# Modulation products moved out of an input phase, a convolution carried on by chunks, and transposes between projection products, in a four-layer Trainium2 kernel

## The reference

```
shift, scale, gate = split(silu(c) @ w_mod + b_mod)
h = rms_norm(x, g) * (1 + scale) + shift
x = x + gate * fn(h)
```

```
b_gate, c_gate, u = split(h @ w_in, 3)
v = c_gate * u
conv[t] = w[2]*v[t] + w[1]*v[t-1] + w[0]*v[t-2]      (per channel)
return (b_gate * conv) @ w_out
```

## Time and profile before

| | |
|---|---|
| median of 3 runs | 2230.7 us (2225.03 to 2233.52) |
| the profiled execution: time, span | 2235.24 us, 2233.4 us |
| TensorE busy, mean granted clock | 1965.2 us (88%), 0.916 |
| VectorE busy | 1664.8 us (75%) |
| ScalarE busy | 1143.7 us (51%) |
| DMA | 551.03 MB, mean 247 GB/s |

### The profile page before, as it was taken

One profiled execution on the slowest core, in us unless ns is written; L12 is line 12 of the kernel. 1 busy time (PEld: TensorE's weight loads), 2 busy tenths in 40 slices (PEclk: granted clock), 3 DMA queues, 4 the chain that ended last, 5 costly groups with the idle time before them and its releaser, 6 DMA issues.

```text
span 2233.4 us, 29567 instructions
## 1 busy us (share of the span) xinstructions
PE 1965.2 (88%) x9224; PEld 1633.4 (73%) x9224; DVE 1664.8 (75%) x2294; ACT 1143.7 (51%) x1600; POOL 36.5 (2%) x47
## 2 busy tenths in 40 slices
PE   2968999877799999999999999585779998678998
PEld 2956887656678888888888888564768877466886
DVE  7877666967498989898898989675676668566554
ACT  2434444333277777777777777424344443434443
POOL 2000000000000000000000000000000000000000
PEclk9988999876699999999999999786689998679999
DMA  7965873964189999999999999373457866435662
GB/s 266 363 204 187 263 250 121 335 201 164 57 287 339 368 337 364 336 350 354 340 362 338 366 337 368 134 248 91 134 178 260 261 209 207 112 112 160 216 208 85
DMA packets 368358, 551.03 MB, mean 247 GB/s; under 512 B 35715, under 2 KB 292998, under 8 KB 368230
## 3 DMA queue, kind: packets, MB, share of 16 engines
q1 hardware_dynamic: 353120, 542.56, 71.9%
q10 hardware_dynamic: 14278, 6.70, 2.2%
q0 software_dynamic: 832, 0.30, 0.1%
HBM read 548.38 MB, written 1.08 MB: 246 GB/s over the span
## 4 chain that ended last, share of the span: by engine, by line
PE 75%; DVE 14%; DMA 5%; issue 3%; ACT 2%; SPq 0%; ACTq 0%; POOL 0%; DVEq 0%; POOLq 0%
PE ps L381 21%; PE ps L383 21%; PE ps L382 21%; PE ps L773 2%; DVE mod_acc L1370 2%; PE ps L919 2%; DVE units_low L376 2%; DMA raw_units<-in_w_in 1%; PE ps L827 1%; PE ps L762 1%; PE ps L750 1%; DMA raw_units<-in_attn_w_qkv 1%; DVE x_tokens L1396 1%; DMA raw_units<-in_conv_w_in 1%; DVE x_normed L1395 1%
## 5 line engine op out<-in xcount | busy, mean ns | idle before, releaser
L376 DVE TENSOR_TENSOR units_low<-raw_units,units_high 128x1024 fp32r<-128x1024 f32 (+2 forms) x840 | 983.5, 1219 | 213.1 <-ACT units_high L372 207.7
L372 ACT ACTIVATE units_high<-raw_units 128x1024 fp32r<-128x1024 f32 (+2 forms) x840 | 845.3, 1057 | 355.0 <-PE ps L383 230.4
L381 PE MATMUL ps<-units_high,hT_high 128*128 128x512 f32 (+2 forms) x1592 | 636.5, 400 | 70.4 <-DVE units_low L376 30.1
L382 PE MATMUL ps<-units_low,hT_high 128*128 128x512 f32 (+2 forms) x1592 | 631.6, 397 | 0.0
L383 PE MATMUL ps<-units_high,hT_low 128*128 128x512 f32 (+2 forms) x1592 | 631.3, 397 | 0.0
L381 PEld LDWEIGHTS ps<-units_high,hT_high 128*128 128x128 f32 (+1 forms) x1592 | 306.4, 192 | 141.0 <-issue 38.1
L383 PEld LDWEIGHTS ps<-units_high,hT_low 128*128 128x128 f32 (+1 forms) x1592 | 305.3, 192 | 67.2
L382 PEld LDWEIGHTS ps<-units_low,hT_high 128*128 128x128 f32 (+1 forms) x1592 | 306.0, 192 | 65.9
L381 PE MATMUL ps<-units_high,aT_high 128*128 128x512 f32 x616 | 252.5, 410 | 0.0
L1370 DVE SCALAR_TENSOR_TENSOR mod_acc<-mod_in,silu_c,mod_acc 128x1024 f32<-128x1024 f32 x192 | 243.9, 1280 | 6.2 <-DMA mod_in<-in_mod_w 3.2
L382 PE MATMUL ps<-units_low,aT_high 128*128 128x512 f32 x616 | 242.9, 394 | 0.0
(11 more groups left out here) (229 smaller groups left out, 1570.0 us busy)
## 6 DMA issues: line engine op xcount, KB each, us to landing
raw_units<-in_moe_w_gate SPq DMA_DIRECT2D x352, 256.0 KB, 4.4
raw_units<-in_moe_w_up SPq DMA_DIRECT2D x352, 256.0 KB, 5.6
raw_units<-in_moe_w_down SPq DMA_DIRECT2D x176, 512.0 KB, 6.1
mod_in<-in_mod_w SPq DMA_DIRECT2D x96, 512.0 KB, 5.8
mod_in<-in_w_mod SPq DMA_DIRECT2D x96, 512.0 KB, 5.5
raw_units<-in_w_gu SPq DMA_DIRECT2D x176, 256.0 KB, 3.3
raw_units<-in_w_down SPq DMA_DIRECT2D x44, 512.0 KB, 4.1
raw_units<-in_w_in SPq DMA_DIRECT2D x32, 512.0 KB, 8.5
```

Of the source, the lines that this page charges most:

```text
L372: eng.activation(whi[:rows, n % H, 0:width], raw[:rows, n % R, 0:width], ACT.Copy).then_inc(f.hi, 1)
L376: eng.tensor_tensor(low[:rows, n % R, 0:width], raw[:rows, n % R, 0:width], whi[:rows, n % H, 0:width].bitcast(F32), ALU.subtract).then_in ...
L381: pe.matmul(dst, ah, bh, start=start, stop=False, **kw)
L382: pe.matmul(dst, ah, bl, start=False, stop=False, **kw)
```

## The change

- **Convolution.** VectorE applies taps on four chunks, one tap after each of the splits 20, 21 and 22; the v of block 4 is made after split 20. The first four chunks get high and low parts of their own, in `aT_high` and `aT_low`, as soon as they are gated; the last four follow in two pairs. `project_out` starts on the first four and waits for `s_cve` before it overwrites the banks of block 5. `sum_gate(0)` stands inside the projection (after unit 2), `sum_cols(1)` behind it. No products before split 5; 20 are spread over splits 5 to 19 (`CONV_MODS`), 4 follow the output splits. SyncE issues six units before the first of their loads.
- **Products.** The first feed-forward now carries 48 (block 1's gate, block 2's columns and gate, block 3's columns), spread over 52 units from unit 7 on; the dilated attention's input phase carries none. In the later feed-forwards 24 and 8 are spread over 52 units from unit 7. Their loads stand two units later in SyncE's queue. Block 2's gate and block 3's columns have accumulators of their own, in parts of `qkT` and `prob`. `sum_cols(3)` follows `sum_cols(2)` behind the feed-forward.
- **Transposes.** In the dilated attention, `sum_gate(2)` stands after block 1, the q transposes after the first unit of block 4, the k transposes after the second unit of block 5, with their evictions. In the second mixers the key copies follow the norm and rotation after the second block, the first four of seven pairs are transposed after unit 14 of 16, `sum_gate` uses banks 0 and 1.

```diff
-MOD_OVER_FFN = 4 + (STEPS - 1) * STEP_UNITS - 2 * FK
+MOD_FFN_FROM, MOD_FFN_OVER, MOD_SP_LATER = AHEAD + 2, 52, 2
+CONV_MODS = [0] * AHEAD + [(4 * k + 4) // 3 - (4 * k) // 3 for k in range(15)] + [0] * (24 - AHEAD - 15)
+SP_LATER = 6
...
 # SyncE
-        phase(fa, N_CONV_IN, 24, blocks(g["conv_w_in"][0], 512), between=MOD_IN_CONV)
-        phase(fa, N_CONV_OUT, 8, rows_of(g["conv_w_out"][0]))
+        for k in range(32):
+            issue_unit(sp, fa, N_CONV_IN, k, 0, conv_in(k) if k < 24 else conv_out(k - 24))
+            if k >= SP_LATER:
+                mods(CONV_MODS[k - SP_LATER + AHEAD] if k - SP_LATER + AHEAD < 24 else 1 if k < 29 else 0)
         phase(fa, N_FFN0, FFN_UNITS, ffn_source(g["ffn_w_gate"][0], g["ffn_w_up"][0], g["ffn_w_down"][0]),
-              between=MOD_GATE + MOD_COLS)
-        phase(fa, N_QKV1, 24, blocks(g["attn_w_qkv"][0], 480), between=MOD_GATE + MOD_COLS)
+              between=2 * (MOD_GATE + MOD_COLS), later=MOD_FFN_FROM + MOD_SP_LATER)
+        phase(fa, N_QKV1, 24, blocks(g["attn_w_qkv"][0], 480))
...
 # TensorE
-        sum_gate(0)
-        sum_cols(1)
-        project_out(fa, N_CONV_OUT, DC, P, lambda k: (s_cyT, 1))
+        project_out(fa, N_CONV_OUT, DC, P, lambda k: (s_cyT, 1 if k < 4 else k // 2), conv=True)
+        sum_cols(1)
...
+            if gate == 1:
+                sum_cols(3)
...
-        project_in(fa, N_QKV1, 6, 480, 2, 0)
-        pe.wait_ge(s_htl, HT(3))
-        sum_gate(2)
-        sum_cols(3)
-        qk_transposes(0)
+        def queries():
+            pe.wait_ge(s_mga, 3)
+            pe.wait_ge(s_q, 1)
+            qk_transposes(0, 0, 4)
+        def keys():
+            pe.wait_ge(s_q, 2)
+            qk_transposes(0, 4, 8)
+        project_in(fa, N_QKV1, 6, 480, 2, 0, {(1, 3): gate2, (4, 0): queries, (5, 1): keys})
...
+            project_in(fb, n0 + N_IN2, 4, 512, s, q0, {(3, 2): first_pairs})
+            sum_gate(s)
+            qk_transposes(1 + l, 4, 5)
+            pe.wait_ge(s_qa, q0 + 4)
+            pe.wait_ge(s_qd, q0 + 4)
+            qk_transposes(1 + l, 5, 7)
+            pe.wait_ge(s_mga, s + 1)
...
 # ScalarE
+        highs(fa, N_CONV_OUT, 0, 2)
+        y_high(aTh[:, :, :, :].rearrange("p a k s -> p (a k s)"), 0, 4, 1)
+        highs(fa, N_CONV_OUT, 2, AHEAD)
+        ac.wait_ge(fa.used, N_CONV_OUT)
+        for c in (4, 6):
+            y_high(hTh[:, c:c + 2, :].rearrange("p a b -> p (a b)"), c, 2, c // 2)
+        highs(fa, N_CONV_OUT, AHEAD, 6)
         mod_gate(0)
-        ac.wait_ge(s_cvd, 2)
-        ac.wait_ge(fa.used, N_CONV_OUT)
-        ac.activation(hTh[:, 0:DC, :].rearrange("p a b -> p (a b)"), cT, ACT.Copy).then_inc(s_cy, 1)
-        highs(fa, N_CONV_OUT, AHEAD, 8)
+        highs(fa, N_CONV_OUT, 6, 8)
...
 # VectorE
+        for k in range(AHEAD, 24):
+            split_low(ve, fa, N_CONV_IN + k)
+            mods(CONV_MODS[k])
+            if k == 20:
+                conv_v(4)
+            if 20 <= k < 23:
+                conv_tap(22 - k, 0)
+        conv_gate(0, 4)
+        lows(fa, N_CONV_OUT, 0, 1)
+        conv_low(yTl, yTh, 0, 4, 1)
+        lows(fa, N_CONV_OUT, 1, 2)
+        conv_v(5)
+        conv_tap(2, 4)
+        lows(fa, N_CONV_OUT, 2, 3)
+        conv_tap(1, 4)
+        lows(fa, N_CONV_OUT, 3, 4)
+        conv_tap(0, 4)
+        conv_gate(4, 2)
+        conv_gate(6, 2)
+        lows(fa, N_CONV_OUT, 4, AHEAD)
+        conv_low(hTl[:, 4:6, :], hTh[:, 4:6, :], 4, 2, 2)
+        conv_low(hTl[:, 6:8, :], hTh[:, 6:8, :], 6, 2, 3)
         lows(fa, N_CONV_OUT, AHEAD, 8)
+        mods(MOD_IN_CONV - sum(CONV_MODS))
...
-                    mods(spread(between, MOD_OVER_FFN, k))
+                    mods(spread(between, MOD_FFN_OVER, k - MOD_FFN_FROM))
```

More of the change, by code:

```diff
@@ L451, in mods, with phase @@
             mod_at[0] += n
-        def phase(f, n0, count, src, it=0, rows=P, between=0, moe_end=0):
+        def phase(f, n0, count, src, it=0, rows=P, between=0, moe_end=0, later=0):
             for k in range(count):
                 issue_unit(sp, f, n0, k, it, src(k), rows, moe_end)
-                mods(spread(between, min(count, MOD_OVER_FFN), k))
+                mods(spread(between, MOD_FFN_OVER if count == FFN_UNITS else count, k - later))
         def blocks(w, width):
@@ L550, in mods_done @@
+        zero_cols(1)
+        zero_gate(1)
+        zero_cols(2)
+        for m in range(3, 8):
+            zero_gate(m)
+            if m < 7:
+                zero_cols(m + 1)
     def mods_done(m, gate):
@@ L653, in conv_in, with project_out @@
                 last.then_inc(fa.used, 1)
-        def project_out(f, n0, chunks, rows, ready):
+        def project_out(f, n0, chunks, rows, ready, conv=False):
+            yTh, yTl = (v[:, :, :, :].rearrange("p a k s -> p (a k) s") for v in (aTh, aTl))
             def unit(k, t, half):
                 n = n0 + k
+                high, rest = (yTh, yTl) if conv and k < 4 else (hTh, hTl)
                 return product(pe, ps[:, 2 * t + half, :],
-                               hTh[0:rows, k, t * P:(t + 1) * P], hTl[0:rows, k, t * P:(t + 1) * P],
+                               high[0:rows, k, t * P:(t + 1) * P], rest[0:rows, k, t * P:(t + 1) * P],
                                whi[0:rows, n % H, half * 512:(half + 1) * 512],
@@ L701, in project_in, with qk_transposes @@
                     last.then_inc(f.used, 1)
[L703 removed]
+                    if (b, kpair) in beside:
+                        beside[b, kpair]()
+        def qk_transposes(a, first, end):
             second = a > 0
[L706 to L712 removed]
+            for nth in range(first, end):
+                pair = PAIRS[a][nth]
+                b = TRANS_BEFORE[a] + nth
+                if nth >= 4:
                     pe.wait_ge(s_qte, b - 3)
@@ L1275, in _, with transposed @@
             k = AHEAD
+            def transposed(first, end):
+                for nth in range(first, end):
+                    pair = PAIRS[1 + l][nth]
+                    ac.wait_ge(s_qtp, TRANS_BEFORE[1 + l] + nth + 1)
+                    ac.activation(qkT[:, 2 * pair:2 * pair + 2, :].rearrange("p a b -> p (a b)"),
+                                  ps[:, 4 + nth % 4, :], ACT.Copy).then_inc(s_qte, 1)
             for b in range(4):
@@ L1568, in _ @@
         hT_low(0)
-        mods(sum(spread(MOD_IN_CONV, 24, i) for i in range(AHEAD)))
         cT = qkv[:, 2048:4096].rearrange("p (c s) -> p c s", c=DC)
@@ L1610, in _, with conv_tap @@
-        ve.wait_ge(s_cvd, 2)
-        ve.wait_ge(s_cy, 1)
-        ve.tensor_tensor(hTl[:, 0:DC, :], cT, hTh[:, 0:DC, :].bitcast(F32), ALU.subtract).then_inc(s_cyT, 1)
+        def conv_tap(tap, c0):
+            for c in range(c0, c0 + 4):
+                w = cols[:, V_CONV + 8 * tap + c:V_CONV + 8 * tap + c + 1]
+                if tap == 2:
+                    ins = ve.tensor_scalar(cT[:, c, :], vT[:, c, 2:S + 2], w, None, ALU.mult)
+                else:
+                    ins = ve.scalar_tensor_tensor(out=cT[:, c, :], in0=vT[:, c, tap:tap + S], scalar=w,
+                                                  in1=cT[:, c, :], op0=ALU.mult, op1=ALU.add)
+                ins.then_inc(dch, 1)
+            chain[0] += 4
+            ve.wait_ge(dch, chain[0])
@@ new lines, in conv_v @@
+        def conv_v(nb):
+            ve.wait_ge(s_cva, 8)
+            ve.wait_ge(fa.used, N_CONV_IN + 4 * nb + 4)
+            for i in range(2):
+                c = 4 * (nb - 4) + 2 * i
+                last = ve.tensor_tensor(vT[:, c:c + 2, 2:S + 2],
+                                        ps[:, 2 * (nb % 2) + i, :].rearrange("p (c s) -> p c s", c=2),
+                                        cT[:, c:c + 2, :], ALU.mult)
+                if i == 0:
+                    last.then_inc(dch, 1)
+            last.then_inc(s_cve, 1)
+            chain[0] += 1
+            ve.wait_ge(dch, chain[0])
+            ve.wait_ge(s_cve, nb - 3)
@@ L1623, in _ @@
         mod_cols(2)
+        mod_cols(3)
         hT_low(2, after=last_two(fa, N_QKV1, 960))
-        mods(sum(spread(MOD_GATE + MOD_COLS, 24, i) for i in range(AHEAD)))
         ve.wait_ge(s_rot[1], 1)
```

220 lines of the change are left out of this document (113 added, 107 removed).

## The result

The changed kernel took 2196.9 us (median of 4 runs, 2191.1 to 2199.1) against 2232.1 for the kernel before on the same chip: ratio 0.9836, 95% interval 0.9808 to 0.9864. It is 35 us faster, where 51 were forecast; 2181 was predicted, in a range of 2167 to 2203, and within 8 us of 2181 with a chance of 0.56; it is 16 away. So the two profiles differ by 44, and the medians by 35: 9 of the missing 16 us are the distance of profiled executions from their medians, and 7 are to be found between the two traces.

A forecast was written before the change was run, and what follows sets the result against it. TensorE was taken to bound the kernel, with 75% of the chain, so its gaps were sought: 14.4 + 13.3 - 1 + 24.3 + 0 = 51 us gained, giving 2181 us, range 2167 to 2203.

The forecast's parts named there:

- The convolution: Convolution stage: output projection starts at 121.4 instead of 141.2, residual done at 151.8 against 166.2; gain 14.4, bounds 10 and 18.
- T: End of block 4 (units 16 to 19) of the convolution's input products on TensorE, forecast at 108.4 us.
- The feed-forward's first step: TensorE's pause in each two-tile feed-forward shortens and slow matmuls go: 5.5, 5.5 and 2.3, together 13.3, bounds 7.8 and 13.5.
- The term of the last layer: Last layer's feed-forward, first step: one product goes, 1.2, and six slow matmuls, 1.2; gain 2.3.
- The body: First feed-forward's body takes 24 products more, 48 over 52 units; loss 1, bounds 0 and 8.
- The rival of capped transfers: Feed-forward body: transfers cap at the experts' 349 GB/s, 6 us, some 10 with late products; total 2190; chance 0.13.
- The second column sum: Behind the first feed-forward: 3.6 us more, offset by transposes at full clock; 0 net, bounds -1 and +1.
- The input phase: Dilated attention's input phase: without products, first scores at 452.4 to 453 instead of 477.2; gain 24.3, bounds 16 and 25.
- The second mixers: Input phases of the last two layers: key copies and transposes moved earlier; gain 0 each, bounds -2 and +1.
- gaps left in the input phase: Rival, attention input phase: late rotations or evictions, two cold restarts, half the gain lost; total 2193; chance 0.15.
- VectorE's backlog beyond the forecast: Rival, convolution: VectorE's chain of splits, taps and roundings loses another 8; total 2189; chance 0.12.

The follow-up runs named there:

- e4: Changed kernel with the convolution block as before the change on all engines; 2211.3 us, ratio 0.989 to the kernel before.
- e5: Changed kernel with feed-forward products spread over 60 units from unit 0, their loads no longer later in SyncE's queue; 2209.7 us, ratio 0.9889 to the kernel before.
- e2: Kernel before, with only the two new clears and their bias loads added on GpSimd at the start; 2236.6 us, ratio 1.001 to the kernel before.
- e1: Changed kernel run once more, nothing edited; 2194.6 us, ratio 0.9823 to the kernel before.
- e6: Changed kernel with block 2's gate and block 3's column products back in the attention input phase, without the two start clears; 2209.6 us, ratio 0.9886.
- e7: Changed kernel with the dilated attention's gate sum and all 32 transposes behind the last value products; 2195.1 us, ratio 0.9821 to the kernel before.
- e8: Changed kernel with both second mixers as before: key copies, gate sum and transposes behind the last block; 2191.0 us, ratio 0.9804 to the kernel before.
- e3: Changed kernel with the two new clears and their bias loads moved behind the first gate sum; 2194.2 us, ratio 0.9814 to the kernel before.
- e11: Changed kernel with early clears, convolution products all before the output splits, block 3's column sum before the scores, key copies behind block 3's splits; 2186.8 us, ratio 0.9787.

## Why the prediction was right, and where it was too large

**The convolution** (14.4): 14.5 between the profiles, 15 when undone alone (e4). The sequence behind T held to half a microsecond.

**The feed-forward's first step** (13.3): 3.7 + 5.6 + 2.1 and, in the first layer, the slow matmuls' 2.2, which hide in the next stage: body without them 187.7 - 2.2 - 6.2 = 179.3, measured 179.6 and 179.2. e5 takes it back, with 7.7, 5.2 and 1.9. The term of the last layer is in part luck: the kernel of e2 has the same pause of 2.5 there, but no slow matmuls behind it, and the stage took 196.6 instead of 198.0. So 1.2 of the 2.1 hang on a clock that falls in some executions and not in others.

**The body** (loss 1): nothing. 179.2 us with 24 products or with 48. The rival of capped transfers, at 349 GB/s, is refuted for this stage: 378 at the top, no wait of TensorE.

**The second column sum** (0, bounds -1 and +1): this is a step that failed. I counted the 3.6 us against a faster set of transposes behind it. In eight profiles with two sums in a row the transposes start 8.7 to 11.4 us after the first sum's start, in five with one sum 6.2 to 6.4: 2.5 to 5.2 lost, by how far the clock has come down. The second batch took 5.3 to 7.0 in all eight; the first kept 3.6 to 3.7 in five of them and took 4.3 to 4.7 in three, e1 among them.

**The input phase** (24.3): 25.0. e6 and e7 split it: products alone 20 (94.7 against 74.5, with the transposes inside), the transposes' place nothing once the products are gone, and 4.7 while they are there (99.4 before, 94.7 in e6). My sum gave the place no term of its own; its end of 452.4 holds either way.

**The second mixers** (0 each): 0.8 and -0.3. The pause grew to 8.74 as forecast. The total of e8, 3.6 lower without this part of the change, leaves open whether it costs something in the heads behind it.

**Not in the sum at all:** the two clears at the start, -3.5. The sum names the accumulators in the change and prices only their column sums; the clears stand in it at nothing, without a reason. I hold 2.7 of it as shown for the first products (e2, e3). In the totals the clears are not clear of noise: 2.1 in e2, 0.4 in e3. The rest of the 3 to 5 at the column sum goes with the transfers from 14 to 44 us, which ran at 332 and 319 GB/s in the kernel before, 275 and 276 in the changed kernel, and 306 with late clears, where the products had started in time. Why these differ stays open. With SyncE's new order and no early clears the column sum stood at 39.8 and 39.9 (e3, e6), with the old order at 37.1 and 38.9, so the order may cost a microsecond of its own.

**The last attention**, -2.3: open. Three profiles without the change gave 116.9 to 117.7, ten with it 117.6 to 121.9, with TensorE at a lower mean clock where it is longer. No edit tried governs it; one kernel with the change is at 117.6. The third layer's heads, the same kind of stage, spread as widely and not upwards: 120.2 to 120.3 in the three, 118.6 to 121.4 in the ten, so chance is a rival here.

Of the rivals, gaps left in the input phase and VectorE's backlog beyond the forecast did not show. The total lies nearer to the times of these rivals (2189 to 2193) than to 2181, but not for their reasons. The rest of the miss, 9 us in the first comparison and 4 in that of e1, is no term that the traces show: both pairs of profiled executions are 44 apart, the medians 35 and 40. Where the executions that were not profiled take longer is not known. Undone one at a time, the three parts cost 16.6, 15.1 and 15.0 us, together more than the 39.9 of the whole; e5 holds more than its part, the 4 in the convolution and twice the products in the first layer.

## What to carry to other kernels

- When a change adds an accumulator, price its clearing and bias load on the engine that makes them and on its neighbour. Here 2.8 us of clears on GpSimd, at a time when VectorE does short copies, started the first products 2.8 us later; the totals showed 2.1 (e2) and 0.4 (e3) of it.
- Products moved from a stage that VectorE bounds to one that TensorE bounds are free as long as VectorE is not the bound there; here it was busy up to 18.4 of 20 us. Put them behind the first step, and their loads too, since a load that waits for a slot holds the weights behind it in SyncE's order.
- Put tiny matmuls into a wait, one batch at a time, rather than two batches in a row: the same 32 cost 2.5 to 5.2 us behind another batch, and about 1 in a wait (e11, one profile).

## What the runs showed of the hardware

- 32 one-column matmuls take 3.63 us at full clock; the next 32 right behind took 5.3 to 7.0 in eight profiles, the granted clock falling to 0.64 (changed kernel, first profile) or 0.50 (e1) meanwhile. A pause of 1.4 us before the second step left the clock up, one of 4.5 to 5.1 did not; one of 2.5 in the last layer was followed by six matmuls 0.43 apart in three profiles and by none in a fourth (e2).
- VectorE's two small tensor_scalar instructions (128x32) took 2.58 us beside a clear of 2048 columns on GpSimd, 0.52 alone, nearly all of it in the second of them; splits and products on 1024 columns beside such a clear (e3) were not slowed.
- The same instructions of a stage bound by short matmuls and hand-overs took 117.6 or 120.8 us, as the granted clock averaged 0.71 or 0.65.
